# Scores of the first head taken from products without the norm, four modulation tiles and one norm on GpSimd and ScalarE, and another first round of places

## The reference

```python
mod = silu(c) @ w_ada + b_ada                  # 6 x 1024: shift1, scale1, gate1, shift2, scale2, gate2
h = rms_norm(x, norm1_w) * (1 + scale1) + shift1
# attention and convolution branches of h, joined as y_mix
x = x + gate1 * (y_mix @ w_out)
h2 = rms_norm(x, norm2_w) * (1 + scale2) + shift2
x = x + gate2 * peer_ffn(h2, ...)

def peer_ffn(h):                               # 8 heads, 16384 experts of one neuron each
    q = h @ peer_wq                            # 8 heads x 2 halves x 128
    s = einsum('bqhpd,hpnd->bqhpn', q, peer_subkeys)
    vals, idx = top_k(s, 16)                   # in each half, then the best 16 of the 16 x 16 sums
    g = softmax(top_s)
    a = gelu(einsum('bqhkd,bqd->bqhk', peer_u[expert], h))
    return einsum('bqhk,bqhkd->bqd', g * a, peer_v[expert])
```

## Time and profile before

| | us |
|---|---|
| median of 3 runs | 1158.65 |
| lowest and highest of them | 1158.63, 1160.64 |
| the profiled execution, on the device | 1159.03 |
| its span in the trace | 1157.0 |
| PE busy | 1044.9 (90%) |
| DVE busy | 853.4 (74%) |
| ACT busy | 704.6 (61%) |
| POOL busy | 345.2 (30%) |

### The profile page before, as it was taken

The page is one execution under the profiler, slowest core; times in us unless marked ns, Lnnn a source line. Parts: engine busy times, 40 slices in busy tenths (PEclk is TensorE's granted clock), DMA queues, the critical chain, the costliest instruction groups (busy, mean ns, idle before and its releaser), DMA issues.

```text
span 1157.0 us, 13373 instructions
## 1 busy us (share of the span) xinstructions
PE 1044.9 (90%) x4675; PEld 725.0 (63%) x4675; DVE 853.4 (74%) x1535; ACT 704.6 (61%) x1393; POOL 345.2 (30%) x367
## 2 busy tenths in 40 slices
PE   8999999999898978788877877799999999999997
PEld 6999987554454423333333323399888888888885
DVE  6998988766667666766677776546677768886776
ACT  3635835866776766666676666661458555577451
POOL 1001005555453544544544544555000000400000
PEclk9999999999999989988988998989999999999999
DMA  9987859999999999999999999999954654455540
GB/s 371 407 333 293 344 221 399 422 421 421 421 421 421 421 421 422 420 422 418 421 404 423 422 416 421 422 419 420 363 209 167 244 186 178 173 192 184 204 157 37
DMA packets 59557, 390.00 MB, mean 337 GB/s; under 512 B 6882, under 2 KB 7906, under 8 KB 15715
## 3 DMA queue, kind: packets, MB, share of 16 engines
q0 software_dynamic: 36864, 268.45, 55.9%
q1 hardware_dynamic: 21152, 120.10, 27.5%
q10 hardware_dynamic: 1474, 0.60, 0.2%
HBM read 388.08 MB, written 1.05 MB: 336 GB/s over the span
## 4 chain that ended last, share of the span: by engine, by line
PE 55%; DMA 28%; ACT 8%; DVE 6%; issue 2%; SPq 0%; POOL 0%; ACTq 0%; DVEq 0%; POOLq 0%
DMA rows<-in_peer_uv,work 17%; PE aux L1701 15%; DMA low_pairs<-in_peer_uv,work 8%; PE pj L1758 6%; PE pj L1760 6%; PE pj L1759 5%; PE pj L1816 5%; PE pj L1817 3%; PE aux L1707 3%; PE pj L1417 2%; ACT rows L1231 2%; PE pj L1419 2%; PE pj L1418 2%; PE aux L1676 2%; DVE rows L2230 2%
## 5 line engine op out<-in xcount | busy, mean ns | idle before, releaser
L1701 PE MATMUL aux<-rows,work 128*128 128x512 f32 x504 | 243.6, 633 | 46.2 <-ACT work L1247 46.0
L1701 PEld LDWEIGHTS aux<-rows,work 128*128 128x128 f32 x504 | 99.9, 202 | 178.1 <-issue 115.6
L1701 PE MATMUL aux<-low_pairs,work 128*128 128x512 f32 x356 | 176.0, 643 | 37.5 <-ACT work L1247 37.5
L992 POOL DMA_INDIRECT rows<-in_peer_uv,work x146 | 140.8, 964 | 231.0 <-PE aux L1701 148.4
L1231 ACT ACTIVATE rows<-rows 128x1024 f32<-128x1024 f32 x134 | 141.1, 1053 | 90.9 <-DVE rows L2230 90.5
L1701 PEld LDWEIGHTS aux<-low_pairs,work 128*128 128x128 f32 x356 | 71.6, 206 | 134.8 <-issue 84.1
L769 DVE TENSOR_TENSOR wlo<-wring,whi 128x1024 fp32r<-128x1024 f32 x98 | 121.0, 1250 | 32.6 <-ACT whi L763 31.8
L1231 ACT ACTIVATE low_pairs<-low_pairs 128x1024 f32<-128x1024 f32 x97 | 102.0, 1052 | 62.2 <-DVE low_pairs L2230 62.0
L992 POOL DMA_INDIRECT low_pairs<-in_peer_uv,work x101 | 97.3, 963 | 122.5 <-PE aux L1701 106.6
L763 ACT CAST whi<-wring 128x1024 fp32r<-128x1024 f32 x98 | 101.4, 1050 | 51.1 <-PE pj L1817 26.4
L2230 DVE TENSOR_TENSOR rows<-rows,aux 128x1024 f32<-128x1024 f32 x66 | 80.0, 1219 | 52.1 <-DMA rows<-in_peer_uv,work 51.6
(11 more groups left out here) (343 smaller groups left out, 2059.3 us busy)
## 6 DMA issues: line engine op xcount, KB each, us to landing
wring<-in_w SPq DMA_DIRECT2D x74, 1024.0 KB, 5.0
rows<-in_w_ada SPq DMA_DIRECT2D x46, 512.0 KB, 9.3
rows<-in_w SPq DMA_DIRECT2D x3, 1024.0 KB, 11.5
rows<-in_peer_uv,work POOLq DMA_INDIRECT x146, 12.7
low_pairs<-in_w SPq DMA_DIRECT2D x2, 1024.0 KB, 7.3
work<-in_late_rows SPq DMA_DIRECT2D x2, 1024.0 KB, 9.2
xT<-in_gate_rows SPq DMA_DIRECT2D x2, 1024.0 KB, 8.2
rows<-in_norm_rows SPq DMA_DIRECT2D x2, 1024.0 KB, 7.0
```

The lines of the kernel that those rows point to most:

```text
L992: pool.indirect_dma_start(out=pair(n), out_offset=None, in_=a["peer_uv"], in_offset=bass.IndirectOffsetOnAxis(ap=expert[g % EXPERTS][:, j: ...
L1701: ins = mm(peer_sum[t][:, half(c)], diag[:, n % PICKS, :], pair(n)[:, D + c * 512:D + (c + 1) * 512], start=(n % (EXPERT_HEADS * PICKS) == ...
```

## The change

It has four parts.

1. **Head 0's scores for tile 0.** ScalarE makes `xg` = `xT` times the gain while the chunks of the residual come, with the shift as a 129th column of each chunk. PE multiplies `xg` with the query weights of head 0 (`query_products`: the first four chunks ahead of the last sums of squares, the rest behind tile 0's), so that a query is known up to the token's factor 1/root, and the shift's part stands in its own column. The scores of both parts are made apart, and VectorE joins them with a factor for each token (`rtok`, from `rstd_by_token`): `scores_of_head_0`.
2. **The norm of tile 0 and tile 1.** VectorE scales tile 0 in one instruction of 128 x 1024. Tile 1 is multiplied with its gain by ScalarE and with 1/root by GpSimd in one instruction, ahead of the first gather in GpSimd's program. ScalarE's `shift(0)` now stands behind the copies of head 0, and PE's four filling matmuls became five at another place.
3. **Modulation tiles.** Tiles 44 to 47 are multiplied with `silu(c)` by GpSimd (128 x 1024, both inputs in SBUF) and summed by ScalarE (`ada_sum`): two sums between the residual chunks, two behind `shift(1)`. VectorE no longer takes them.
4. **Places.** The first round has 12 places (`low` 0 in place of `low` 7), in another order: `rows` 1 comes as the seventh and waits for the four sums.

```diff
-PLACES = [("rows", 0), ("rows", 1), ("low", 2), ("low", 3), ("low", 4), ("low", 5), ("rows", 2), ("rows", 3), ("rows", 4), ("rows", 5), ("ring", 0), ("low", 7)]
-ROUNDS = [11] + [12] * 5 + [11] * 3
+PLACES = [("rows", 0), ("rows", 1), ("low", 2), ("low", 3), ("low", 4), ("low", 5), ("rows", 2), ("rows", 3), ("rows", 4), ("rows", 5), ("ring", 0), ("low", 0)]
+FIRST_ROUND = (0, 2, 3, 4, 5, 11, 1, 6, 7, 8, 9, 10)
+ROUNDS = [12] * 5 + [11] * 4
+POOL_TILES = (44, 46, 47, 45)
-PLACE_OF = [k for size in ROUNDS for k in range(size)]
+PLACE_OF = [k for n, size in enumerate(ROUNDS) for k in (range(size) if n else FIRST_ROUND)]
...
+            for n in POOL_TILES:
+                if n < RING_TILES:
+                    pool.wait_ge(ada_loaded[ada_place(n)[0]], 16 * (ada_place(n)[1] + 1))
+                else:
+                    pool.wait_ge(last_ada_loaded, 16)
+                pool.tensor_tensor(pool_tile(n), pool_tile(n), cbc, ALU.mult).then_inc(ada_product, 1)
+            pool.wait_ge(second_inv, 2)
+            pool.wait_ge(xg_ready, KC + 2)
+            pool.tensor_tensor(hT[:, :, P:T], hT[:, :, P:T], rstd[:, P:T].unsqueeze(1).broadcast_to([P, KC, P]), ALU.mult).then_inc(h_scaled, KC)
...
                     if n == FIRST_ROUTED:
                         pool.wait_ge(routed, 1)
+                    if n == first_of("rows", 1):
+                        pool.wait_ge(last_ada_used, len(POOL_TILES))
                     if n == first_of("rows", 2):
                         pool.wait_ge(queries, 2)
                     if n == first_of("rows", 3):
-                        pool.wait_ge(last_ada_used, LAST_TILES)
                         gate_diagonals(0)
-                    if n == first_of("low", 7):
-                        pool.wait_ge(queries, 8)
...
             halves_ = [slice(t * P, (t + 1) * P) for t in range(NT)]
+            def gain_x(c):
+                nc.scalar.activation(xg[:, c, 0:P], xT[:, c, 0:P], ACT.Copy, scale=gain[:, c:c + 1]).then_inc(xg_ready, 1)
+            def gain_x_of_tile_1(*chunks):
+                for c in chunks:
+                    ins = nc.scalar.activation(hT[:, c, P:T], xT[:, c, P:T], ACT.Copy, scale=gain[:, c:c + 1])
+                return ins
+            def ada_sum(k):
+                n = POOL_TILES[k]
+                act.wait_ge(ada_product, k + 1)
+                nc.scalar.activation(pool_tile(n), pool_tile(n), ACT.Copy, accum_out=mod[:, n:n + 1]).then_inc(last_ada_used, 1)
             for c in range(KC - 1):
                 act.wait_ge(taken_dve, c + 1)
                 nc.scalar.activation(sq[:, c, :], xT[:, c, :], ACT.Square).then_inc(squares, 1)
+                if c == 0:
+                    nc.scalar.copy(xg[:, :, P:P + 1], mod[:, 3 * KC:4 * KC].unsqueeze(2)).then_inc(xg_ready, 1)
+                if c < KC - 2:
+                    gain_x(c)
                 if c in (1, 3):
                     round_to(31 if c == 1 else 32)
-            act.wait_ge(early_added, 1)
+                if c in (3, 4, 5):
+                    gain_x_of_tile_1(*{3: (0, 1), 4: (2, 3, 4), 5: (5, )}[c])
+                if c in (4, 5):
+                    ada_sum(c - 4)
+            act.wait_ge(taken_dve, KC)
             nc.scalar.activation(sq[:, KC - 1, 0:P], xT[:, KC - 1, 0:P], ACT.Square).then_inc(squares, 1)
-            act.wait_ge(taken_dve, KC)
+            gain_x(KC - 2)
+            gain_x(KC - 1)
+            act.wait_ge(taken_dve, KC + 1)
             nc.scalar.activation(sq[:, KC - 1, P:T], xT[:, KC - 1, P:T], ACT.Square).then_inc(squares, 1)
-            for t, ts in enumerate(halves_):
+            gain_x_of_tile_1(KC - 2, KC - 1).then_inc(xg_ready, 1)
+            def root(t):
                 act.wait_ge(sums, 2 + t)
-                nc.scalar.activation(rstd[:, ts], aux[:, 2 + t, 0:P], ACT.Sqrt, bias=eps[:, 0:1], scale=1.0 / D).then_inc(std_ready, 1)
+                nc.scalar.activation(rstd[:, halves_[t]], aux[:, 2 + t, 0:P], ACT.Sqrt, bias=eps[:, 0:1], scale=1.0 / D).then_inc(std_ready, 1)
             def shift(t):
@@ -1199,13 +1248,17 @@
                 nc.scalar.copy(s_all[:, h + first * EXPERT_HEADS::EXPERT_HEADS, :],
                                aux[:, h % 2, first * 2 * KEYS:].rearrange("p (n k) -> p n k", k=2 * KEYS)).then_inc(scores_out, 1)
+            root(0)
+            for s in range(2):
+                act.wait_ge(early_products, s + 1)
+                nc.scalar.copy(pq[:, 0, s, 0:P + 1], aux[:, 4 + s, 0:P + 1]).then_inc(early_query_out, 1)
+            root(1)
+            act.wait_ge(early_products, 3)
+            nc.scalar.copy(s_all[:, 0, :], aux[:, 1, 0:2 * KEYS]).then_inc(early_query_out, 1)
             shift(0)
-            for s in range(2):
-                act.wait_ge(early_query, s + 1)
-                nc.scalar.copy(pq[:, 0, s, 0:P], aux[:, 4 + s, 0:P]).then_inc(early_query_out, 1)
-            act.wait_ge(early_scores, 1)
-            nc.scalar.copy(s_all[:, 0, :], aux[:, 0, 0:2 * KEYS]).then_inc(early_scores_out, 1)
             shift(1)
+            ada_sum(2)
+            ada_sum(3)
...
             score_query(0)
+            gate_exps(0)
             score_out(0)
-            gate_exps(0)
...
-            def keep_busy(n, b):
-                pe.wait_ge(const_ready, 13)
-                for _ in range(n):
-                    mm(aux[:, b, 0:2 * P], ident[:, :], wsT[:, 0:2, :].rearrange("p g t -> p (g t)"), start=True, stop=True)
...
             out_sums(0, 1, 2, 3)
             whole(mixed_in, 2)
             out_sums(4, 5)
-            out_sums(6, 7)
+            query_of_head_0 = w_slot(FIRST_HEADS[0])
+            w_wait(pe, FIRST_HEADS[0])
+            def query_products(s, chunks):
+                for k in chunks:
+                    pe.wait_ge(xg_ready, k + 2)
+                    ins = mm(aux[:, 4 + s, 0:P + 1], query_of_head_0[:, k, s * P:(s + 1) * P], xg[:, k, :], start=(k == 0), stop=(k == KC - 1))
+                return ins
+            for s in range(2):
+                query_products(s, range(HC))
+            out_sums(6, 7, tiles=(0, ))
+            for s in range(2):
+                query_products(s, range(HC, KC)).then_inc(early_products, 1)
+            out_sums(6, 7, tiles=(1, ))
...
             def early_scores_of_head_0():
-                w_wait(pe, UNITS_1.index(queries_of(0)))
-                w = w_slot(UNITS_1.index(queries_of(0)))
-                for s in range(2):
-                    for k in range(KC):
-                        if s == 0:
-                            pe.wait_ge(h_ready, KC + k + 1)
-                        ins = mm(aux[:, 4 + s, 0:P], w[:, k, s * P:(s + 1) * P], hT[:, k, 0:P], start=(k == 0), stop=(k == KC - 1))
-                    ins.then_inc(early_query, 1)
-                n = UNITS_1.index(keys_of(0))
-                w_wait(pe, n)
+                w_wait(pe, FIRST_HEADS[2])
+                keys = w_slot(FIRST_HEADS[2])
                 for s in range(2):
                     pe.wait_ge(early_query_out, s + 1)
-                    ins = mm(aux[:, 0, s * KEYS:(s + 1) * KEYS], pq[:, 0, s, 0:P], w_slot(n)[:, 0, s * KEYS:(s + 1) * KEYS], start=True, stop=True)
-                ins.then_inc(early_scores, 1)
+                    k = keys[:, 0, s * KEYS:(s + 1) * KEYS]
+                    of_shift = mm(aux[:, 1, s * KEYS:(s + 1) * KEYS], pq[:, 0, s, P:P + 1].broadcast_to([P, P]), k, start=True, stop=True)
+                    ins = mm(aux[:, 0, s * KEYS:(s + 1) * KEYS], pq[:, 0, s, 0:P], k, start=True, stop=True)
+                    if s == 1:
+                        of_shift.then_inc(early_products, 1)
+                ins.then_inc(early_products, 1)
...
-            keep_busy(4, 1)
             early_scores_of_head_0()
-            pe.wait_ge(taken_dve, KC)
+            pe.wait_ge(early_query_out, 3)
+            for _ in range(5):
+                mm(aux[:, 1, 0:2 * P], ident[:, :], wsT[:, 0:2, :].rearrange("p g t -> p (g t)"), start=True, stop=True)
+            pe.wait_ge(taken_dve, KC + 1)
+            pe.wait_ge(h_ready, 2 * KC)
             turn_h2(0)
             pe.wait_ge(h_ready, 3 * KC)
...
-            def last_ada_tiles():
-                dve.wait_ge(last_ada_loaded, 16)
-                for c in range(LAST_TILES):
-                    tile = last_ada[:, c, :]
-                    v.tensor_tensor_reduce(tile, tile, cbc, 1.0, 0.0, ALU.mult, ALU.add,
-                                           mod[:, RING_TILES + c:RING_TILES + c + 1]).then_inc(last_ada_used, 1)
-                dve.wait_ge(ada_used, RING_TILES)
-                dve.wait_ge(last_ada_used, LAST_TILES)
+            def last_ada_bias():
+                dve.wait_ge(ada_used, min(POOL_TILES))
+                dve.wait_ge(last_ada_used, len(POOL_TILES))
                 chain.link(v.tensor_tensor(mod[:, LAST_ADA:], mod[:, LAST_ADA:], cols[:, B_ADA + LAST_ADA:B_ADA + 6 * KC], ALU.add))
...
-            def second_norm():
-                for t in range(NT):
```

(62 more changed lines are left out.)

14 lines of the change are left out of this document (8 added, 6 removed).

## The result

The median of five runs is 1171.55 us against 1158.65, a ratio of 1.0109 (95% interval 1.0097 to 1.012): slower by 12.9 us. The profiled execution took 1171.93, also 12.9 above that of before. The forecast was 1163.2, with 1157.3 to 1165.6 as its range. The direction was right and the size was not: the time lies 6 us above the range.

The account below looks back on a forecast made before the run. Memory bounds the gathers, so the first gather's start decides. Routing 2.9 us later, 0.9 for its addition and 0.8 for PE's clock make +4.6: 1159.03 becomes 1163.6, less 0.38 gives 1163.2; range 1157.3 to 1165.6.

Parts of the forecast that it names:

- What is costed at nothing: ScalarE's sums, late queries and the twelfth place: hidden or covered by 12 places, 29.9 us of stream; no cost.
- holes near 200 to 225: In the gather stream: DMA share under 1.0, holes of 1 to 3 us, if late queries were not covered.
- The turns: GpSimd's products and VectorE's dots and subtractions, both with two SBUF inputs, alternate: 3.4 to 3.45 us a pair.
- PE's start of chunk 6: PE needs piece 30's remainder: starts 1.7 us later, ends chunk 7 at 161.1 in place of 158.9.
- PE's clock: PE stands still some 2.4 us before chunk 5's squares, then runs at the lower clock: 0.8 us added.
- ScalarE's second sum: `ada_sum(1)` on ScalarE, ahead of chunk 6's square: costs 1.05 us, to 165.2, not hidden as chunk 5 is late.
- From the residual to the routing: Chain to head 0's scores: undisturbed, routing begins at 167.45 in place of 169.00, gain 1.55 us; with turns, 171.9.
- The routing's addition: Routing's fifth instruction, two SBUF inputs, meets GpSimd's norm of tile 1 at 172.8 and waits 0.9 us.
- (a): Rival: no long turns or residual under 2 us late, only tile 1's norm delays routing: -0.65, 1158.0; chance 0.29.
- (b): Rival: no turns, join right behind PE's scores, gain 1.9 us and perhaps 0.4 to 0.8 more: 1156.0 to 1156.4; chance 0.12.
- (c): The forecast itself: residual 3 to 4 us late, 1161.2 to 1165.5; chance 0.53.
- longer case: Lower clock through PE's 22 products, up to 2.5 us more, or pieces' starts costing PE twice: up to 1167; chance 0.06.

Follow-up runs that it names:

- e1: The kernel after, with place 1 moved forward one step each round instead of going back at once to natural order: 1163.23 us, ratio 1.004.
- e2: The kernel before with only the new places, first round and order of the kernel after: 1165.71 us, ratio 1.0054.
- e6: e1 with GpSimd's four modulation products cut to their first column, ScalarE's four sums left whole: 1157.77 us, ratio 0.9987.
- e4: e1 with modulation tiles 44 to 47 back on VectorE as dots, GpSimd keeping tile 1's norm: 1157.96 us, ratio 0.9988.
- e8: The kernel before with four extra GpSimd products of 128 x 1024, two SBUF inputs, into unused scratch: 1164.73 us, ratio 1.0049.
- e7: e1 with ten filling matmuls of 128 x 256 on PE ahead of chunk 6: 1162.62 us, ratio 1.0033.
- e3: The kernel before with twelve places in the first round, in the order of e1: 1159.14 us, ratio 1.0001.
- e5: e4 with tile 1's inverse and norm on VectorE behind the first eight picks' routing: 1160.47 us, ratio 1.0011.
- e9: The kernel before with ten GpSimd memsets of 128 x 1024 into unused scratch, in front of the gathers: 1159.73 us, ratio 1.0005.

## Why the prediction was right and wrong

**What failed: "What is costed at nothing", the 12 places.** The text says "the stream has 12 places, 29.9 us, before it must wait for a used place". That counted places, not the distance between two uses of one. In the first round place 1 is seventh; the second round is in natural order, so it is second there, the fourteenth pick, a distance of only seven picks. All other places keep a distance of eleven or more. Seven picks are 7 x 2.49 = 17.4 us of stream, while the seventh pick held its place for 31.7 us, and the row at 217.68 shows the wait: 14.06 us, of which 7.2 are lost to the stream. Nothing of the cost model was missing for this; the two lists in the diff, written beside each other, show it. The prediction read "another order" and asked only what the seventh gather waits for, not who takes its place next. The text even named the sign, holes near 200 to 225, and hung it on the queries. e1 and e2 show the cause from both sides: 1.0109 falls to 1.004 without the order, and the order alone makes 1.0054.

**The first gather: the main mechanism was right, +5.6 instead of +4.6.** Its terms:
- The turns. Forecast pairs of 3.4 to 3.45 us, measured 3.0 to 3.3. The steps of the residual's chunk 5 were to come at 162.7 to 163.1, and the row is at 163.11. e6, e4 and e8 show that the turns cause the lateness.
- PE's start of chunk 6. Forecast 1.7 late, measured 157.26 - 153.06 = 4.2. The order of the turns was another: ScalarE's new products put VectorE's previous subtraction from 145.29 to 145.81, so GpSimd had tile 44 (147.11) 0.24 us ahead of the dot of tile 40 (147.35), and three GpSimd instructions, not two, stood ahead of the remainder of piece 30. In e7, where the tile came 0.3 us behind the dot, the order was the forecast's and the remainder was through at 155.1 to 155.2, where 154.75 was forecast. The text worked out one order only.
- PE's clock. The 0.8 us were put at the squares, behind a standstill of 2.4 us that did not come, as PE reached them only at 165.7; there the clock was 0.93 to 1.00. The low clock came ahead, in chunks 6 and 7, behind the wait of 4.03 us, and made them 8.6 us in place of 5.85. So PE and not VectorE was the last for the seventh chunk: 165.94, where about 163.5 was forecast.
- ScalarE's second sum. Forecast in the path, to 165.2 (the text counts three products with the gain ahead of it, the traces show two, and 165.2 is the sum with two). In the kernel after it ended at 165.6, before the late seventh chunk, and cost nothing; in e7 the forecast's case came about.
- From the residual to the routing. Forecast 171.9 - 163.6 = 8.3, measured 7.5. Part 1 is worth 9.9 - 7.5 = 2.4 us and not 1.55: of the 0.8 more, 0.5 are PE's: the eight products took 1.79 (x16 with their loads) where 2.12 were taken, and the four sums 0.89 where 1.06. The 2.4 hold for part 1 with the norms of part 2.
- The routing's addition, forecast 0.9 late, measured 1.32 - 0.23 = 1.1.

The sum by the measured terms is 6.8 - 2.4 + 1.1 = 5.5, as found. So the forecast was near by offsetting errors: the residual came 2.3 later than forecast, against 0.8 for the clock and 0.8 in part 1 the other way. That e1, without the order, measured 1163.23 where 1163.2 was forecast is luck in the same sense.

**The rivals.** (a), no long turns, fell: it is e4 or e6, and would have been 1158. (b) had the better size for part 1, 2.3 to 2.7. The start by itself fits (c)'s own range: 1158.65 + 5.6 = 1164.2. Its longer case had the clock too low in PE's 22 products, where it was 0.93 to 1.00; a low clock did lengthen the path, in chunks 6 and 7. **What held:** the memory bounds the stretch between first and last gather, microsecond for microsecond (e1: 4.4 late at the start, 4.1 in the time), as long as the start is not ahead of 171; the twelfth place is worth nothing (e3); ScalarE's sums are hidden where the residual is on time (e6).

## What to carry to other kernels

When buffers are taken round and round and the order of one round is changed, list for each buffer the distance to its next use; the smallest one sets the depth of the whole stream, whatever their number. Work moved to an idle GpSimd is not free if it reads two SBUF inputs while VectorE has such instructions too: count the turns, and place it where VectorE reads PSUM or waits. Here 2.4 us of dots taken off VectorE put some 8 us of turns in front of it. A faster chain to the start of a stream pays only as long as its consumers, too, are ready earlier: e5 starts 2.8 us earlier than before and is slower. And an added filler can be in the way of the work that it is to help (e7), so look when that work was ready.

## What the runs showed of the hardware that was not expected

- A wait for the shared inputs can hit a very small instruction in full: GpSimd's products of one column took 1.13 us in e6 (0.19 where VectorE had nothing going), the rest of a VectorE instruction of 1.2 us.
- After a standstill of 4 us PE's granted clock stayed at 0.50 for 6 us in the kernel after and for 3 in e1, with the same program up to there. The first gathers of the two executions lie 1.2 us apart; no such spread was counted in the forecast.
- Ten memsets of 128 x 1024 took 1.0 us each on GpSimd while VectorE's instructions with two SBUF inputs ran beside them, and held none of these up (e9).
